# Low parts of 52 weight tiles a layer by an accumulating DMA onto ScalarE's negated high part, in place of a GpSimd subtraction

## The reference

```python
def peer(h, w_query, sub_keys, u_tab, v_tab):      # h (512, 1024), w_query (1024, 2048)
    q = (xt @ w_query).reshape(T, 8, 2, 128)       # 16 tiles of 1024 x 128
    s = jnp.einsum('thpd,hpnd->thpn', q, sub_keys) # sub_keys (8, 2, 128, 128)
    s_half, i_half = lax.top_k(s, 16)
    cand_s = s_half[:, :, 0, :, None] + s_half[:, :, 1, None, :]
    ...                                            # the best 16 of 256 pairs: ids; gates = softmax
    a = gelu(einsum('chkd,cd->chk', u_tab[idc], xc))     # u_tab (16384, 1024)
    y = einsum('chk,chkd->cd', gates * a, v_tab[idc])    # v_tab (16384, 1024)
```

## Time and profile before

| | us |
|---|---|
| median of 3 runs | 3664.95 (3655.76 to 3673.56) |
| span of the profiled execution | 3662.8 |
| PE busy | 3550.3 (97%) |
| DVE busy | 3128.9 (85%) |
| ACT busy | 1581.8 (43%) |
| POOL busy | 1393.5 (38%) |

### The profile page before, as it was taken

One profiled execution on the slowest core, in us unless ns is written; L12 is line 12 of the kernel. 1 busy time (PEld: TensorE's weight loads), 2 busy tenths in 40 slices (PEclk: granted clock), 3 DMA queues, 4 the chain that ended last, 5 costly groups with the idle time before them and its releaser, 6 DMA issues.

```text
span 3662.8 us, 61258 instructions
## 1 busy us (share of the span) xinstructions
PE 3550.3 (97%) x19206; PEld 3257.2 (89%) x19206; DVE 3128.9 (85%) x6312; ACT 1581.8 (43%) x2335; POOL 1393.5 (38%) x1140
## 2 busy tenths in 40 slices
PE   6999999999999999999999999999999999999999
PEld 5766788999999989999977667789999999999999
DVE  6899877999899878888868997779998987888888
ACT  4474434444455433333345644334444454333333
POOL 0000003575565534454500000036765655444543
PEclk9999999999999999999999999999999999999999
DMA  5111263467999899999921112635689999999998
GB/s 194 60 52 58 81 252 111 140 196 256 338 349 331 297 321 340 353 342 349 332 86 58 52 64 95 244 104 159 192 295 342 333 328 301 355 349 343 349 345 284
DMA packets 408601, 863.49 MB, mean 236 GB/s; under 512 B 165520, under 2 KB 231056, under 8 KB 407952
## 3 DMA queue, kind: packets, MB, share of 16 engines
q1 hardware_dynamic: 297456, 539.62, 44.2%
q0 software_dynamic: 73728, 268.47, 20.9%
q10 hardware_dynamic: 37152, 52.45, 3.9%
HBM read 774.41 MB, written 85.98 MB: 235 GB/s over the span
## 4 chain that ended last, share of the span: by engine, by line
issue 50%; PE 28%; POOL 17%; DMA 2%; DVE 2%; POOLq 0%; SPq 0%; ACT 0%; DVEq 0%; ACTq 0%
PE ps L829 8%; PE ps L830 8%; PE ps L831 8%; POOL w_lo L512 7%; POOL gbuf L528 5%; POOL spare L542 4%; PE ps L579 2%; PE ps L580 2%; PE ps L578 2%; DMA raw<-stream 1%; PE ps L803 1%; DMA cg<-gelu_scratch 1%; DMA gbuf<-u_rows,ids_u 0%; DVE oneR L1730 0%; DVE w_lo L1767 0%
## 5 line engine op out<-in xcount | busy, mean ns | idle before, releaser
L893 ACT CAST w_hi<-raw 128x1024 fp32r<-128x1024 f32 x680 | 715.8, 1055 | 871.0 <-DMA raw<-stream 821.5
L578 PE MATMUL ps<-h_hi,w_hi 128*128 128x384 f32 (+1 forms) x2944 | 1063.8, 361 | 3.5 <-DVE qT L1459 1.4
L580 PE MATMUL ps<-h_hi,w_lo 128*128 128x384 f32 (+1 forms) x2944 | 1037.7, 352 | 0.0
L579 PE MATMUL ps<-h_lo,w_hi 128*128 128x384 f32 (+1 forms) x2944 | 1036.4, 352 | 0.0
L829 PE MATMUL ps<-cf_hi,w_hi 128*128 128x384 f32 x2048 | 692.5, 338 | 13.2 <-DVE w_lo L1767 6.9
L830 PE MATMUL ps<-cf_lo,w_hi 128*128 128x384 f32 x2048 | 690.6, 337 | 0.0
L831 PE MATMUL ps<-cf_hi,w_lo 128*128 128x384 f32 x2048 | 690.5, 337 | 0.0
L542 POOL TENSOR_TENSOR spare<-spare 128x1 f32<-128x1 f32 x504 | 347.7, 690 | 851.6 <-DVE y_sp L1746 491.0
L578 PEld LDWEIGHTS ps<-h_hi,w_hi 128*128 128x128 f32 x2944 | 555.0, 189 | 58.2 <-issue 16.2
L579 PEld LDWEIGHTS ps<-h_lo,w_hi 128*128 128x128 f32 x2944 | 555.0, 189 | 38.9 <-issue 5.7
L580 PEld LDWEIGHTS ps<-h_hi,w_lo 128*128 128x128 f32 x2944 | 554.1, 188 | 37.5
(11 more groups left out here) (247 smaller groups left out, 4923.8 us busy)
## 6 DMA issues: line engine op xcount, KB each, us to landing
raw<-stream SPq DMA_DIRECT2D x682, 512.0 KB
gelu_scratch<-g_out ACTq DMA_DIRECT2D x256, 192.0 KB
cg<-gelu_scratch SPq DMA_DIRECT2D x256, 192.0 KB
c_scratch<-stage SPq DMA_DIRECT2D x64, 512.0 KB
cg<-c_scratch SPq DMA_DIRECT2D x256, 128.0 KB
qT<-ada SPq DMA_DIRECT2D x32, 512.0 KB
cgate<-ada SPq DMA_DIRECT2D x32, 512.0 KB
w_rows<-ada SPq DMA_DIRECT2D x32, 512.0 KB
```

What stands on the lines that cost most here:

```text
L578: nc.tensor.matmul(ps[:, b, 0:n], wh, hi[:, c, t0:T], start=c == 0, stop=False)
L579: nc.tensor.matmul(ps[:, b, 0:n], wh, lo[:, c, t0:T], start=False, stop=False)
L580: mm = nc.tensor.matmul(ps[:, b, 0:n], wl, hi[:, c, t0:T], start=False, stop=c == C - 1)
L893: nc.scalar.copy(w_hi[:, s], raw[:, s]).then_inc(hi_done, 1)
```

## The change

For tiles 72 to 123 of each layer (the last 12 of the query and U0 to U39), the low part no longer is a subtraction on POOL. ACT, right after the cast of tile i+2, writes minus the high part to a new buffer `w_add` (1024 columns, four slots; a second set of four from tile 100 on). POOL waits for that, runs a one-column operation that orders it, and issues a DMA that adds `raw` onto `w_add` in place: raw + (-high). PE multiplies from `w_add`, and waits for the slot's count `lo_added` instead of `lo_done`. POOL still subtracts for tiles 68 to 71. DVE waits for all four `lo_added` counts before U40, and adds 52 to `lo_done`. PE's loop over U0 to U39 is cut in two at U16 (tile 100).

```diff
+ADDED_FIRST, ADDED_MOVE = 72, 100
+ADDED_END = I_U + U_ROUTE
+ADDED_EACH = (ADDED_END - ADDED_FIRST) // 4
...
+        w_add = [at("w_add0", sq_base, [P, 4, C, P], F32R), at("w_add1", base + 74 * KB, [P, 4, C, P], F32R)]
...
+                def add_raw(i):
+
+                    pool.wait_ge(asked, l * (ADDED_END - ADDED_FIRST) + i - ADDED_FIRST + 1)
+                    pool.wait_ge(neg_done, l * (ADDED_END - ADDED_FIRST) + i - ADDED_FIRST + 1)
+                    nc.gpsimd.tensor_tensor(spare[:, 31:32], spare[:, 17:18], spare[:, 18:19], ALU.add).then_inc(asked, 1)
+                    nc.gpsimd.dma_start(w_add[i >= ADDED_MOVE][:, i % 4].bitcast(F32), raw[:, i % 4],
+                                        accum_op=ALU.add).then_inc(lo_added[i % 4], 16)
...
-                with pool.Fori(I_QRY // 4, I_U // 4) as r:
-                    for s in range(4):
-                        low(s, l * NT + 4 * r + s)
+                for i in range(I_QRY, ADDED_FIRST):
+                    low(i % 4, l * NT + i)
+                for i in range(ADDED_FIRST, I_U):
+                    add_raw(i)
...
-                    low(u % 4, l * NT + I_U + u)
+                    add_raw(I_U + u)
...
-                    pe.wait_ge(lo_done, g + 5)
+                    w_low, at_low, count = low or (w_lo, lo_done, g + 5)
+                    pe.wait_ge(at_low, count)
...
+                def negative(i):
+
+                    act.wait_ge(hi_done, l * NT + i + 1)
+                    nc.scalar.mul(w_add[i >= ADDED_MOVE][:, i % 4], w_hi[:, i % 4].bitcast(F32), -1.0).then_inc(neg_done, 1)
...
                 for i in range(I_QRY, I_U):
                     high_at(i + 2)
+                    if i + 2 >= ADDED_FIRST:
+                        negative(i + 2)
...
                     high_at(I_U + u + 2)
+                    if u + 2 < U_ROUTE:
+                        negative(I_U + u + 2)
...
-                dve.wait_ge(lo_done, l * NT + I_U + U_ROUTE + 4)
+                for s in range(4):
+                    dve.wait_ge(lo_added[s], (l + 1) * ADDED_EACH * 16)
+                dve.wait_ge(lo_done, l * NT + ADDED_FIRST + 4)
+                nc.vector.memset(spare[:, 0:1], 0.0).then_inc(lo_done, ADDED_END - ADDED_FIRST)
```

More of the change, by code:

```diff
@@ L301, in build_trunk @@
         lo_done = sem("lo_done")
+        neg_done = sem("neg_done")
+        lo_added = [sem(f"lo_added{s}") for s in range(4)]
         tile_done = sem("tile_done")
@@ L398, in build_trunk @@
         room = sem("room")
+        asked = sem("asked")
         a_gelu = sem("a_gelu")
@@ L504, in _ @@
             nc.gpsimd.memset(spare[:, 20:21], 0.0).then_inc(room, 1)
+            nc.gpsimd.memset(spare[:, 31:32], 0.0).then_inc(asked, 1)
             nc.gpsimd.memset(spare[:, 15:20], 0.0).then_inc(lo_done, 4)
@@ L564, in read_no, with added, product @@
                     return l * (NE // 2) + i // 2 + 2
-                def product(s, g, e, hi, lo, ready=None, chunks=None, t0=0):
+                def added(i, r):
+                    return w_add[i >= ADDED_MOVE], lo_added[i % 4], (l * ADDED_EACH + r + 1) * 16
+                def product(s, g, e, hi, lo, ready=None, chunks=None, t0=0, low=None):
                     b, n = s % 2, T - t0
@@ L572, in product @@
                     pe.wait_ge(bank_read[b], e)
-                    pe.wait_ge(lo_done, g + 5)
+                    w_low, at_low, count = low or (w_lo, lo_done, g + 5)
+                    pe.wait_ge(at_low, count)
                     for c in range(C):
-                        wh, wl = w_hi[:, s, c], w_lo[:, s, c]
+                        wh, wl = w_hi[:, s, c], w_low[:, s, c]
                         if chunks is not None:
@@ L599, in proj @@
                 def proj(i, hi, lo, chunks=None):
-                    product(i % 4, l * NT + i, l * (NE // 2) + i // 2 + 1, hi, lo, chunks=chunks)
+                    product(i % 4, l * NT + i, l * (NE // 2) + i // 2 + 1, hi, lo, chunks=chunks,
+                            low=added(i, (i - ADDED_FIRST) // 4) if i >= ADDED_FIRST else None)
                 def proj_loop(i0, i1, hi, lo, ready=None):
@@ L789, in u_tiles @@
                             product(s, l * NT + I_U + u0 + 4 * r + s,
-                                    l * (NE // 2) + (I_U + u0) // 2 + 2 * r + s // 2 + 1, h_hi, h_lo, t0=P)
+                                    l * (NE // 2) + (I_U + u0) // 2 + 2 * r + s // 2 + 1, h_hi, h_lo, t0=P,
+                                    low=added(I_U + u0 + s, (I_U + u0 - ADDED_FIRST) // 4 + r))
                 def u_tile(u):
@@ L805, in c_group @@
                         mm.then_inc(c_mm, 1)
-                u_tiles(0, U_ROUTE)
+                u_tiles(0, ADDED_MOVE - I_U)
+                u_tiles(ADDED_MOVE - I_U, ADDED_END - ADDED_MOVE)
                 g = 0
```

## The result

The changed kernel takes 3760.3 us (median of 4 runs, 3752.0 to 3769.6) against 3660.4 for the kernel before (4 runs, 3655.2 to 3673.6): a ratio of 1.027, 95% interval 1.024 to 1.030. It is 100 us slower. The forecast was 3740, with 3662 to 3845 as its range.

A forecast was written before the change was run, and what follows sets the result against it. PE was taken as the bound, busy 3550.3 of 3662.8 us. Adding 64 us for late low parts and 12 for exponentials, less 1 at U40, gave a 3738 span, so a 3740 median; range 3662 to 3845.

The forecast's parts named there:

- P: POOL's time to issue a tile's transfer, one-column operation included: taken as 1.9 us, 1.3 at best, 3.3 where DVE holds it.
- D: Time of the accumulating transfer after its issue: taken as 5.6 us, between 3.8 and 8.4.
- the 12 us for the exponentials: Four times a layer ACT's table load and exponential delay the cast; 1.5 us each, 8 x 1.5 = 12.
- negation: ACT's added multiplication of 1024 columns a tile, writing minus the high part: taken as 1.1 us, between 1.05 and 1.3.
- P + D against 4.9: Issue plus transfer, 7.5 us, against 4.9 left between the negated part and the product needing it: 2.6 late.
- time of a tile: In U0 to U39, 2.6 us late over a three-tile chain adds 0.87: one tile every 5.0 us, from 4.16.
- U0 to U39, two layers: Lateness over this stretch: 37 tiles x 2 layers x 0.87 us = 64 us added.
- DMA share: Sign expected in the profile after: the DMA engines' share in U0 to U39 at 0.8 or more.
- rival 1: It fits: issue plus transfer about 5 us, PE stands at most at the exponentials; 3665, up to 3683; chance 0.18.
- Rival 2: DMA engines set U0 to U39's pace: 6.0 us a tile, 3813; in part, 3757 to 3770; 0.28 shared with Rival 4.
- rival 3: Faster: DVE's 25 us a layer carry on past U40, removing PE idle time there; at best 3647; chance 0.03.
- Rival 4: DVE holds POOL's ordering operation or issue at worst, 3.3 us every time: 3776; chance 0.28 shared with Rival 2.

The follow-up runs named there:

- plain: The changed kernel with the transfer as a copy of raw onto the buffer, nothing added: 3700.2 us, ratio 1.0108.
- lowlast: The changed kernel with PE issuing a tile's 16 high-part matmuls first, then waiting, then the 8 with the low part: 3715.4 us, ratio 1.0157.
- plain_lowlast: The changed kernel with the transfer copying instead of adding, and PE's 8 low-part matmuls of a tile moved last behind the wait: 3671.1 us, ratio 1.0031.
- eighth: The changed kernel with the transfer cut to 128 of the 1024 columns, 64 KB: 3686.9 us, ratio 1.0071.

## Why the prediction came out as it did

The side and the range were right, and the median missed by 20 us of a loss of 100. The sum had the right mechanism and left out another, the slower matmuls behind each stand. That it still came near is in part luck: P was too high and D too low by about as much, and the 12 us for the exponentials, which never came, stood in for part of the 28 us that were missing.

| step | predicted | measured |
|---|---|---|
| negation | 1.1 (1.05 to 1.3) | 1.06 |
| P, issue | 1.9 (1.3 to 3.3) | 1.3 mostly, 3.2 at worst |
| D, transfer | 5.6 (3.8 to 8.4) | 6.3 median, 4.8 to 8.0 |
| P + D against 4.9 | 7.5 | 7.6 |
| time of a tile | 5.0 | 5.4 |
| U0 to U39, two layers | +64 | +94 |
| exponentials | +12 | none seen |
| DMA share | 0.8 or more | 0.95 |
| query | 0 | 0 |

**P and D.** P was sized too high. The issue itself was never held for long: 857 to 1099 ns for all 104, and 0.86 at 707.45 beside DVE's two-input operation (in the run plain one began at 698.89, inside such an operation that ran from 698.46 to 700.78, and took its usual 0.57). The prediction had quoted the Trainium skill, SBUF — State Buffer, "Who interferes with whom", that descriptor generation needs only the write interface and a tensor_tensor doesn't hold it; the rows agree. The one-column operation ahead of it does read SBUF, and it was held, 2.33 us at 700.52. The same section of the Trainium skill says that a DVE instruction with two inputs in SBUF contends with a GpSimd instruction that reads SBUF, and this row agrees. D was sized too low by 0.7. Its lower bound, 3.8, was too low for an addition: the shortest of all 104 landed after 4.5. The estimate of rival 1 from the Trainium skill, DMA: Bandwidth & Descriptors, "Anatomy of one DMA — SWDGE (gpsimd) path", 2.0 us plus bytes at 436 GB/s, gave 3.2. The copy's 2.9 is near it; the addition's 4.8 in the same stretch is not, and the rule doesn't hold for it.

**The step that failed is from lateness to time a tile.** 2.6 us late over three tiles gave 0.87 us a tile, 64 us in all; measured were 94, or 1.2 a tile. Two things lay under it, and the sum had neither. First, *the clock*: lateness was priced as standing time only, but 19 of the 94 us are the lower clock behind waits, and 9 more the restarts of the matmul pipeline. The earlier trace rows showed the clock at 1.00, where PE never stood; nothing at this place in the trace of before showed its fall. Second, *full engines*: a load came late too (17.5 us of casts' waits in layer 1), which lengthens another part of the chain. With the low parts due later, full engines by themselves still hold a tile to 4.85 us (lowlast), 51 of the 94 us. That PE stood 66 us where the sum had 64 doesn't confirm the sum: with a product of 4.54 us, as PE was busy for one, the same chain closes at (4.54 + 3.4 + 7.6) / 3 = 5.18 us a tile, an estimate, and leaves 50 us of standing. Late loads and uneven landings are there to make up the rest, but no run measures them apart.

**Rival 2 was half right, and its price in part by luck.** "If only a part of it counts, 5.3 us a tile, 92 us" is what the span shows. Its ground was a transfer of 3.66 us of the engines; it took 2.9 (the sum's 1.83 was off on the other side). By the shares that would be 1.83 + 0.52 + 2.9 = 5.25 us a tile, yet lowlast, with engines as full, does a tile in 4.85: the shares of packets in flight overlap, as the prediction had warned. The chain, the clock and the restarts make up what lies between 4.85 and 5.4. The limits overlap: later due low parts give back 45 us (lowlast), leaving out the addition, which shortens both the chain and the engines' time, 60 (plain), both together 89 (plain_lowlast), of 100.

**The exponentials' 12 us.** The step "with the chain late it adds 1.5 each" failed. noexp makes the exponentials copies, without a table load, and nothing came back. A likely reason, which no run shows by itself, is that the wait of these tiles overlaps a late transfer or a late load.

**Rival 1** fails by D and by full engines; **rival 3**, faster, by what was said against it: DVE waits 27.4 us at U40. Its two-input operations of 2048 columns all take 2.29 us now, as predicted, which is the 25 us; in all DVE gained 40 us a layer, since others got shorter too (a cast of 256 columns 0.29 instead of 1.51 us on average), and this is worth nothing. PE's idle time in the 468.5 us behind U39 is 7.9 and 9.6 us, where it was 9.6 and 8.8. **Rival 4** occurs for single tiles only.

## What to carry to other kernels

Work moved from an elementwise engine onto a DMA is not free: price its latency in the chain that feeds the bound engine, and its time on the 16 engines against what the loads leave over, each by itself, and expect trouble if either is within a few tenths of its limit. Judge the chain by its slow landings, not by its median. If TensorE is the bound and will stand for some 2 us at a time, add to the standing time what the lower clock and the restarts take behind it, here 28 us on 66; and when an operand comes late, first try to let the products that don't need it go ahead, which cost nothing here and gave back 45 us of 100.

## What the runs showed of the hardware

- An accumulating transfer within SBUF of 512 KB took 4.8 us to land in the query's stretch, where all else took 0.3 of the DMA engines' time, and 3.0 us of all 16 engines; a copy of the same bytes 2.9 and 1.3. From U0 to U39 the shares give 2.9 and 1.5. Its issue on POOL took 0.87 us against 0.57. At 64 KB an addition lands in 2.3 us at least (eighth), so some 2 us are fixed, and the other 2.5 go with the bytes.
- Matmuls started 0.32 instead of 0.17 us apart for some 3 us after PE had stood 1.9 us in the midst of dense work; 11 episodes of lower clock took 19 us. In eighth, whose waits for the transfer were 1.7 us at most, the granted clock was 1.00 in every window of 1 us from U0 to U39 of both layers.
- Half the transfers brought the clock lower than all of them (0.91 against 0.96 in layer 1; both 0.95 in layer 2), with fewer and longer stands of PE.
- A one-column operation on POOL whose operands lie in SBUF took 0.18 us, and up to 2.33 where it fell beside DVE's operation with two inputs in SBUF; the issue of a transfer was not held there. With the subtractions gone from POOL, DVE's work of U0 to U39 took 119 instead of 160 us.
